# A two-block transformer on one core: the first modulation in split form, and the scan tables moved beside the first attention

## The reference, cut to what matters

```python
silu_c, silu_cc = jax.nn.silu(c), jax.nn.silu(c_ctx)
for l in range(2):
    shift, scale, gate = jnp.split(silu_c @ w_mod[l] + b_mod[l], 3, axis=-1)
    shift_c, scale_c, gate_c = jnp.split(silu_cc @ w_mod[l] + b_mod[l], 3, axis=-1)
    n = rms_norm(h, pre_norm_g[l]) * (1.0 + scale[:, None]) + shift[:, None]
    nc = rms_norm(hc, pre_norm_g[l]) * (1.0 + scale_c) + shift_c
    p, pc = n @ w_in[l], nc @ w_in[l]          # q, k, v, gates of the four kinds of heads
    ...                                        # attention, output projection, residual
# second block: h_t = lam_bar * h_{t-1} + b_bar * u_t with a complex lam_bar = exp(lam * dt)
```

## Time and profile before

| What | us |
|---|---|
| median of three executions | 3105.8 |
| the profiled execution, its own time | 3112.07 |
| its span | 3110.3 |
| PE busy | 2926.6 |
| DVE busy | 1937.8 |
| ACT busy | 1164.8 |
| POOL busy | 354.0 |

### The profile page before, as it was taken

How to read it: one execution, slowest core, us unless ns; L and a number is a source line. 1 busy time by engine, 2 the same in 40 slices (tenths; PEclk the granted TensorE clock), 3 DMA queues, 4 the chain that set the end, 5 groups by cost and what they waited for, 6 DMA issues and landing times. The chain is left out here.

```text
span 3110.3 us, 40412 instructions
## 1 busy us (share of the span) xinstructions
PE 2926.6 (94%) x15557; PEld 2367.4 (76%) x15557; DVE 1937.8 (62%) x3393; ACT 1164.8 (37%) x1870; POOL 354.0 (11%) x317
## 2 busy tenths in 40 slices
PE   7989899999989997999999999989999999999998
PEld 2447677787767775868787777755789999999886
DVE  3238778676777767462445557875866666666444
ACT  3233332323323334242433443333344444444443
POOL 5760000000000000000000003532400000000000
PEclk9999999999999998999999998985899999999999
DMA  9846246353344564333333454420244555555554
GB/s 337 277 147 233 96 139 203 104 172 107 123 141 163 191 235 159 132 100 106 117 114 109 138 169 139 137 93 19 90 149 152 181 183 190 184 180 189 194 191 154
DMA packets 154592, 484.79 MB, mean 156 GB/s; under 512 B 17168, under 2 KB 18192, under 8 KB 153232
## 3 DMA queue, kind: packets, MB, share of 16 engines
q1 hardware_dynamic: 139968, 439.42, 42.2%
q10 hardware_dynamic: 14432, 42.79, 4.0%
HBM read 469.03 MB, written 13.11 MB: 155 GB/s over the span
## 5 line engine op out<-in xcount | busy, mean ns | idle before, releaser
L1484 DVE TENSOR_TENSOR split_weights<-common,split_weights 128x1024 fp32r<-128x1024 f32 x644 | 797.5, 1247 | 599.2 <-ACT split_weights L2211 551.5
L2211 ACT ACTIVATE split_weights<-common 128x1024 fp32r<-128x1024 f32 x644 | 671.4, 1052 | 812.6 <-PE bank L1160 752.1
L1158 PE MATMUL bank<-split_weights,features 128*128 128x512 f32 x1920 | 807.4, 421 | 48.9 <-DVE split_weights L1484 19.5
L1160 PE MATMUL bank<-split_weights,features 128*128 128x512 f32 x1920 | 760.7, 396 | 0.0
L1159 PE MATMUL bank<-split_weights,features 128*128 128x512 f32 x1920 | 760.0, 396 | 0.0
L1158 PEld LDWEIGHTS bank<-split_weights,features 128*128 128x128 f32 x1920 | 367.9, 192 | 163.7 <-issue 48.6
L1160 PEld LDWEIGHTS bank<-split_weights,features 128*128 128x128 f32 x1920 | 367.0, 191 | 80.7
L1159 PEld LDWEIGHTS bank<-split_weights,features 128*128 128x128 f32 x1920 | 368.1, 192 | 78.3 <-issue 11.3
L1607 DVE CUSTOM_DVE_ANT_0 common<-first_block_work,common 128x512 f32<-128x512 f32 x448 | 336.2, 751 | 92.3 <-DMA first_block_work<-w_mod_cols 75.1
L1158 PE MATMUL bank<-ffn_input_split,split_weights 128*128 128x256 f32 (+1 forms) x1376 | 389.8, 283 | 0.8 <-issue 0.8
L1160 PE MATMUL bank<-ffn_input_split,split_weights 128*128 128x256 f32 (+1 forms) x1376 | 389.0, 283 | 0.0
(11 more groups left out here) (295 smaller groups left out, 3396.3 us busy)
## 6 DMA issues: line engine op xcount, KB each, us to landing
common<-w_in SPq DMA_DIRECT2D x260, 512.0 KB, 3.4
common<-w_up SPq DMA_DIRECT2D x172, 512.0 KB, 4.3
first_block_work<-w_mod_cols SPq DMA_DIRECT2D x256, 256.0 KB, 3.8
common<-w_out SPq DMA_DIRECT2D x104, 512.0 KB, 3.3
common<-w_down SPq DMA_DIRECT2D x84, 512.0 KB, 3.4
old_stream<-w_mod SPq DMA_DIRECT2D x64, 512.0 KB, 4.7
trig<-common ACTq DMA_DIRECT2D x32, 272.0 KB, 4.4
second_block_work<-trig ACTq DMA_DIRECT2D x32, 272.0 KB, 2.7
```

The lines of the kernel that those rows point to most:

```text
L1158: e.matmul(out_ap, xs[0], ws[0], start=first, stop=False)
L1160: return e.matmul(out_ap, xs[0], ws[1], start=False, stop=last)
L1484: e.tensor_tensor(lo, raw, hi.bitcast(F32), ALU.subtract).then_inc(*low_done.tick(("lo", m)))
L2211: e.activation(split_slots[:, 0, i, 0:words], raw_slots[:, m % RAW, 0:words], ACT.Copy).then_inc(*high_done.tick(("high", m)))
```

## The change

The mod pieces are put in one list with q's and k's pieces (`first_pieces`), go through the same slots (4 + 8 = 12 in the first stage, `RING`) and are split like them. silu(c) is split too, into four stationary columns (high c, high ctx, low c, low ctx); each half piece then takes two one-pass products (with the weights' high and low part), and a 4 x 2 matrix `pair` adds the rows in `mod_turn`. The row scaling of x, which stood ahead of the first stage, is spread between its first pieces. The small operations are given out two after each mod piece. The tables leave the first stage: `table_steps` gives one step every six ticks of the clock, beginning after the first stage, with three buffers that now hold the Sin in place, and the store of a table one step after its Sin. The loads of layer constants come 10 ticks later.

```diff
+def first_pieces():
+    ready = []
+    for i in range(4):
+        for c in (i, 4 + i):
+            for kg in range(KT // KP):
+                yield "mod", c, kg
+                if kg % 4 == 3 and ready:
+                    yield ready.pop(0)
+        ready = [("in", c, g) for c in range(2) for g in (2 * i, 2 * i + 1)]
+    yield from ready
...
+TABLE_SIDES, TURNS_AFTER = 6, 11
...
+        if self.clock % TABLE_SIDES == 0:
+            self.table()
...
     def whole(self):
         self.do("begin")
+        self.do("split_silu")
+        self.weights()
         self.do("ssm_parameters")
-        for t in range(NT):
-            self.do("scale_rows", 0, t)
-            self.do("rows_scaled", 0, t)
         self.do("steps")
         self.first_stage()
         self.background.append(self.modulation())
+        self.tables = self.table_steps()
...
+        for kind, c, g in FIRST_PIECES:
+            if kind == "in":
+                while c == 0 and g == 6 and small:
+                    self.do(*small.pop(0))
+                self.first_products(q + c, range(LT if c else NT), NT * c, g)
+                continue
+            m = self.take()
+            self.do("mod_products", c, g, m)
+            self.finish_split()
+            done += 1
+            for _ in range(2):
+                if small:
+                    self.do(*small.pop(0))
...
+    def table_steps(self):
+        for j in range(SJ + 2):
+            if j < SJ:
+                self.do("table_angles", j)
+            if 0 <= j - 1 < SJ:
+                self.do("table", j - 1)
+            if j > 1:
+                self.do("table_store", j - 2)
+            yield
...
-                    self.do("load_layer_consts", l, self.scratch)
+                    self.later(10, "load_layer_consts", l, self.scratch)
...
             for k in range(KP):
-                kk = KP * kg + k
-                done = e.matmul(bank[0:2, :], silu_c[:, kk, :], mod_slots[:, w % MOD_SLOTS, k * CH:(k + 1) * CH],
-                                start=kk == 0, stop=kk == KT - 1)
+                kk, words = KP * kg + k, slice(k * CH, (k + 1) * CH)
+                for i, part in enumerate(split_piece(m)):
+                    done = e.matmul(bank[0:4, :], silu_s[:, kk, :], part[:, words], start=kk + i == 0, stop=kk + i == KT)
...
         def table_angles(j):
-            x = trig_x[j % 2]
-            for s, n in seen.new(at("steps"), at("coefficients", "ci"), at("table_made", j - 2) if j > 1 else START):
+            x = trig_x[j % 3]
+            for s, n in seen.new(at("steps"), at("coefficients", "ci"), at("table_stored", j - 3) if j > 2 else at("x_turned", KT - 1)):
```

More of the change, by code:

```diff
@@ L250, in weights @@
             m = self.loaded
-            if m >= RAW and m - RAW not in self.raw_free:
+            if slot_before(m) >= 0 and slot_before(m) not in self.raw_free:
                 return
@@ L267, in take @@
         self.finish_split()
-        while self.split < min(self.pieces, n + HALVES) and self.split < self.loaded:
+        while self.split < self.loaded and self.split < n + HALVES:
             self.do("high", self.split)
@@ L399, in first_stage @@
-        for j in range(step // 2, SJ):
-            self.do("table", j - 1)
-            self.do("table_angles", j)
-        self.do("table", SJ - 1)
-        self.do("tables_end")
-        for piece in pieces:
-            self.first_products(*piece)
-    def mod_load(self):
-        if self.mod_loaded < MOD_PIECES:
-            self.do("mod_load_first", self.mod_loaded)
-            self.mod_loaded += 1
+        q, self.projections = self.projections, self.projections + 2
+        done, small = 0, []
@@ L412, in first_products, with table @@
+    def table_steps(self):
[7 more added lines that the diff above has]
+            yield
+        self.do("tables_end")
+        self.tables = None
+        yield
+    def table(self):
+        if self.tables is not None:
+            next(self.tables)
     def first_products(self, p, tiles, bank, kg):
@@ L503, in finish @@
         def finish(p, t, bank):
+            while g and self.tables is not None:
+                self.table()
             r = self.staged
@@ L984, in build @@
     subln = W.one(HD)
+    steps_row = W.one(T2)
     qk_g = W.two(2, HD)
@@ L999, in build @@
     hss = small.one(HEADS * 2)
+    pair = small.one(2)
     head_sums = [small.one(HEADS) for _ in range(2)]
@@ L1547, in tables_end @@
         def tables_end():
-            for s, n in seen.new(at("table_made", SJ - 1), at("table_stored", SJ - 2), at("table_stored", SJ - 1)):
+            for s, n in seen.new(*(at("table_stored", SJ - i) for i in range(1, 4))):
                 e.wait_ge(s, n)
@@ L2188, in build @@
     trig_loaded = [loading(f"trig{i}_loaded") for i in range(TRIGS)]
-    tables_stored = [loading(f"tables{i}_stored") for i in range(2)]
+    tables_stored = [loading(f"tables{i}_stored") for i in range(3)]
     def scalar_program(e):
@@ L2205, in begin, with split_silu @@
             e.activation(silu_c, c_in, ACT.Tanh, scale=0.5).then_inc(*tables_made.tick(("silu_tanh",)))
+        def split_silu():
+            for s, n in seen.new(at("silu")):
+                e.wait_ge(s, n)
+            e.activation(silu_s[:, :, 0:2], silu_c, ACT.Copy).then_inc(*tables_made.tick(("silu_high",)))
         def high(m):
@@ L2533, in scan_load @@
         def scan_load(j):
-            for s, n in seen.new(at("table_stored", SJ - 2), at("table_stored", SJ - 1),
+            for s, n in seen.new(*(at("table_stored", SJ - i) for i in range(1, 4)),
                                  at("scan_out", j - TRIGS) if j >= TRIGS else START):
```

142 lines of the change are left out of this document (69 added, 73 removed).

## The result

The changed kernel takes 3123.01 us in the median of seven executions (3115.63 to 3129.46), the kernel before 3107.14 on the same chip (seven, 3105.08 to 3113.99). The ratio is 1.0041, 95% interval 1.0029 to 1.0053: slower by 0.4%, 12.7 us. Ratios leave out executions that lie far above the fastest of their kernel: one of the run without angles (3254.9 us) and two of the kernel before. The forecast was 3090 and faster, with a range of 3076 to 3104; the time lies outside it, and above the 3120 of the slowest rivals. The profiled execution took 3122.94 us (span 3121.1). PE was busy 2896.8 us, DVE 2038.6, ACT 1275.1, POOL 385.9: PE is busy 30 us less than before, DVE 101 more and ACT 110 more.

A forecast was written before the change was run, and what follows sets the result against it. PE was taken to bound the first stage, PE and DVE close together behind it. First stage -38 (+5 - 38 - 5) and tables +22 (14 + 3 + 5) gave -16 us: 3096 profiled, 3090 against the median; range 3076 to 3104.

The forecast's parts named there:

- the slowest rivals: Whole kernel: half clock in the rounds, 3120 us, chance 0.05; POOL and DVE excluding each other, 3116 us, chance 0.17.
- The start: Up to the second chunk pair's first matmul: constant delayed 5 us, PE begins near 29, pair ends near 60; +5 us.
- POOL no longer stands in DVE's way here: In the three rounds: with the tables moved, DVE needs 29.5 us a round, undisturbed by POOL.
- The three rounds: From 54.6 to 202.4 us: a round takes 36.5 us, three 109.5 instead of 147.8, a gain of 38.
- The half-clock rival: In the rounds: PE idles at each mod piece and runs at 1.2 GHz, round 46.5 us, 3120 us; chance 0.05.
- The rest of q and k: End of the first stage, 28.0 us: the 6.69 us wait goes, the features' wait grows by about 2; -5 us.
- POOL beside the attention: 230.4 to 431.5 us: POOL's passes lengthen DVE's two-input work, +14 us to triple 195, +3 after it.
- The port rival: Beside the attention: POOL's and DVE's two-input work exclude each other wholly, tables cost 48 us, 3116 us; chance 0.17.
- ACT beside the attention: 317.5 to 431.5 us: Sin, table loads and stores bring ACT to 98 of 114 us; late Exp cost +5.
- The end of +25: Upper end of ACT's cost among the attention's units: Exp's 64.0 us of waits for DVE's maxima can't be filled.
- The first rival (hidden): Beside the attention: idle time of DVE and ACT takes in the tables, which cost 3 us, 3071 us; chance 0.25.
- ACT as a bound of 117 us in 114: In the attention: table switches at 1.91 us give ACT 117 us of work in 114, +25, 3110 us; chance 0.08.

The follow-up runs named there:

- the run without angles: Changed kernel with POOL's four passes per table left out, ACT's Sin and the stores kept: 3100.91 us, 0.9976 of the kernel before.
- the run without Sin: Changed kernel with ACT's 32 Sin left out, POOL's passes and the stores kept: 3107.77 us, 0.9995 of the kernel before.
- with one input: Changed kernel with POOL's last pass per table, a two-input subtraction, made a one-input pass of the same size: 3116.5 us, 1.0029.
- with Sin two behind: Changed kernel with Sin two tables behind the angles instead of one, and four buffers: 3121.53 us, 1.0045.
- the two without POOL's passes: Changed kernel without POOL's table passes: once with ACT's Sin kept, 3100.91 us, once with Sin left out too, 3082.91 us.
- The run with three small steps: Changed kernel with three instead of two small steps (mod_turn, mod_scale, features) after each piece of the first modulation: 3110.0 us, 1.0009.
- the two traces without tables: POOL's passes and Sin left out, stores kept: changed kernel, all 32 tables, 3082.91 us; kernel before, 30 of 32 tables, 3098.53 us.

## Why the prediction was wrong

**The start, +5 forecast, +10.5 measured.** Two errors stand against each other here. I had the constant held back by 5 us and PE beginning near 29. It landed a microsecond earlier than before, and PE began at 23.41:

```profile
13.80 0.23 ACT L2259 ACTIVATE first_block_work<-common 128x32 f32<-128x32 f32 x1 [3.90 <-DMA first_block_work<-consts]
```
```profile
23.41 1.01 PE L1222 MATMUL bank<-split_weights,silu_split 128*4 128x512 f32 x2 [23.41 <-DVE split_weights L1536]
```

Yet the pair ended at 65.1 and not near 60, 41.7 us behind PE's first product instead of 31: DVE worked 41.4 of 49.4 us, and PE waited 1.82 and 4.35 us for `low` and `mod_rows` in the first half and 1.21 and 1.99 in the second. I had counted ACT's queue there and not DVE's. Some 2 us of it are POOL's first tables: triple 0 starts at 70.7 to 71.0 us in the changed kernel and the runs without Sin, with one input and with Sin two behind, at 68.2 and 69.1 in the two without POOL's passes. So "POOL no longer stands in DVE's way here" did not hold for these three.

**The three rounds, -38 forecast, -21.9 measured (147.8 to 125.9).** This is the first step that failed: the overlap. The price of a piece on PE was nearly right (3.86 us for sixteen matmuls, 3.68 forecast) and DVE's 28.8 us a round too (29.5 forecast). Over PE's 31.8 us I allowed 4.7 us for imperfect overlap; the middle round took 40.9, 9.1 more. Two stops for features and one for `low` are 5.0 us. PE was busy 35.9 instead of 31.8: eight products at half clock behind the stops are 1.7 of these 4.1, the mod pieces (15.7 us for 14.7) 1.0, and the rest stays open. The run with three small steps, which brings the features earlier, gave back 9.9 us. The half-clock rival named the right effect at the wrong place: the mod pieces of the rounds ran at full speed but for the first twelve matmuls (5.28 us, where twelve later took 2.93), the q and k products behind a stop did not.

**The rest of q and k, -5 forecast, -8.5 measured.** The wait of 6.69 us went, as forecast; the wait for the features, which I had growing by 2 us, stayed at 3.13.

**POOL beside the attention, +14 and +3 forecast, 13.2 and 3.6 measured** by the run without Sin. Both steps held in place and in the sum, but the sizes agree by some luck: a table cost DVE 1.2 us ahead of the units, not 0.9, and 0.6 behind, not 0.45, and less of it reached the time. Nor did POOL pay as forecast: its two-input pass went from 1.46 to 1.52 us, not above 1.8. The port rival (a table costs DVE 2 us) did not hold.

**ACT beside the attention, +5 forecast, 14.8 measured** by the trace of the run without angles, 14.3 by the time of the one without Sin. This is the second step that failed. I priced ACT by its load in 114 us, which left room, and by how late an Exp may come. The room is there (82.56 of 114.1 us), but the units hang on a serial chain in which DVE waits for ACT's squares of the heads, or for a silu row's tanh, and PE for DVE's combination. At two places the Sin and table loads put ahead of these reached PE, 3.6 and 3.3 us of wait, with half clock behind each. The end of +25 in the text was for another chain, Exp behind DVE's maxima; I took 5. The other 3.4 of the 14.8 us went ahead of the units, where I had counted nothing for ACT. The wait for the angles, which I had not seen, cost nothing that can be seen.

**The cover that was taken for granted.** The tables in the kernel before cost 9.9 us, most of it at `tables_end`, of which the -5 for the rest of q and k was a part. This spoils no term of the sum, but it means that the split form with what goes with it, for which start and rounds had -33, was worth 13.4 us. By the two traces without tables it costs 4.6 us up to triple 0 and gives 15.6 from there to triple 72.

Sum: -23.3 for everything but the tables (forecast -38), +36.0 for these (forecast +22): +12.7. The first rival (hidden) and ACT as a bound of 117 us in 114 fall.

## What to carry to other kernels

Price an instruction that is put into a queue by what stands directly behind it and who waits for that, not by the idle share of its engine: ACT with a quarter of its time free still cost 14 us. Before moving work out of a place because it is "hidden" there, leave it out once at the old place and once at the new; the difference of the two is the price of the move, and here each of the two was misjudged. At the old place the cost was not the sharing but the point where everything waited for the last table. A new consumer in a tuned list needs its inputs given out earlier: one small step more per piece was worth 9.9 us, more than any other single edit that kept the whole computation.

## What the hardware showed

A table load of 1.28 us is all that a switch between Sin and Exp cost: in the run without angles the load at 358.54 us begins 0.02 after the instruction ahead of it ends, the ACTIVATE behind it at 359.84, 0.02 after the load, and 19 loads in 230 us of the changed kernel have a mean of 1283 ns. The Trainium skill, "ScalarE: Activation LUTs", section "What ACT_TABLE_LOAD costs", adds a drain of about 1380 ns to each switch; nothing of it is seen here.

POOL's passes are longer where DVE works more, as DVE's are beside POOL: the two small ones went from 0.587 us to 0.833 in the attention and 1.112 in the split stage, the table from 4.7 us to 5.5 and 6.0.

Two short stops stood ahead of a fall of the clock. In the run with three small steps PE had worked for 35 us without a stop, waited 0.86 us up to 108.73, ran three products at 0.39 to 0.47 us, waited 1.48 us up to 111.15, and then its products took 0.63 us (1.2 GHz) until 114.3, after which they had 0.39 again (2.4 GHz). In the changed kernel the single wait of 1.16 us up to 126.08 was followed by products of 0.39 us. The stretches, with the granted clock third from the end:

```profile
108.70:111.70 3.00, 1.48 (x4) 0.99 (x5) 2.40 (x4) 1.07 (x3) 0.00 (x0) 0.87 0.79 289
111.70:114.70 3.00, 3.00 (x9) 2.32 (x8) 1.61 (x2) 3.00 (x6) 0.00 (x0) 0.56 0.43 167
114.70:117.70 3.00, 3.00 (x15) 2.29 (x14) 2.04 (x3) 0.46 (x1) 0.00 (x0) 1.00 0.50 176
```
